# Two inputs also laid out features by tokens, and the memory's norm moved behind its projections

## What is computed

```python
for l in range(DEPTH):                                   # DEPTH = 2
    x = x + hybrid_mixer(rms_norm(x, norm_mix[l]), w_in[l], ...)
    x = x + memory_cross_attention(rms_norm(x, norm_mem_q[l]),
                                   rms_norm(mem, norm_mem_kv[l]), w_mem_q[l], w_mem_kv[l], w_mem_o[l])
    x = x + conv_ffn(rms_norm(x, norm_ffn[l]), ...)
# memory_cross_attention: q = h @ w_q; k, v = split(mem_n @ w_kv); softmax(q k^T) v @ w_o
# rms_norm(x, g) = x * rsqrt(mean(x*x) + 1e-6) * g
```

## Time and profile before

| what | us |
|---|---|
| median of 3 runs | 1925.69 |
| lowest, highest | 1925.57, 1926.07 |
| profiled execution, device time | 1925.96 |
| its span, first to last instruction | 1924.1 |
| PE busy in the span | 1901.3 |
| DVE, ACT, POOL busy | 1436.3, 1158.2, 397.0 |

### The profile page before, as it was taken

The page is one execution under the profiler, slowest core; times in us unless marked ns, Lnnn a source line. Parts: engine busy times, 40 slices in busy tenths (PEclk is TensorE's granted clock), DMA queues, the critical chain, the costliest instruction groups (busy, mean ns, idle before and its releaser), DMA issues.

```text
span 1924.1 us, 30347 instructions
## 1 busy us (share of the span) xinstructions
PE 1901.3 (99%) x11612; PEld 1656.2 (86%) x11612; DVE 1436.3 (75%) x2539; ACT 1158.2 (60%) x2120; POOL 397.0 (21%) x442
## 2 busy tenths in 40 slices
PE   9999999999999999999999999999999999999999
PEld 8878998887899988888887788888888898878887
DVE  5866986576698759875786978866885677888874
ACT  6666765565677546555667556555554666756552
POOL 1110222011012103420122204411440102122430
PEclk9999999999999999999999999999999999999999
DMA  8434556543455655655552355555565544345553
GB/s 298 139 104 142 196 188 233 181 134 124 140 165 193 201 187 176 195 191 172 189 173 99 111 164 197 192 191 184 189 193 191 187 155 151 105 137 182 191 190 128
DMA packets 90689, 329.93 MB, mean 171 GB/s; under 512 B 10032, under 2 KB 10416, under 8 KB 90288
## 3 DMA queue, kind: packets, MB, share of 16 engines
q1 hardware_dynamic: 90544, 327.98, 51.8%
HBM read 326.89 MB, written 1.05 MB: 170 GB/s over the span
## 4 chain that ended last, share of the span: by engine, by line
PE 86%; DVE 7%; ACT 4%; issue 1%; DMA 1%; SPq 0%; POOL 0%; DVEq 0%; ACTq 0%
PE PS L83 84%; PE PS L86 2%; DVE WL L98 2%; ACT TMP L95 2%; ACT WH L92 1%; DVE TMP L108 1%; DVE SM L114 1%; DMA RAW<-wts 1%; DVE X L98 0%; DVE SM L108 0%; ACT M L92 0%; ACT TMP L92 0%; DVE SM L98 0%; ACT M L95 0%; SPq L80 0%
## 5 line engine op out<-in xcount | busy, mean ns | idle before, releaser
L98 DVE TENSOR_TENSOR WL<-RAW,WH 128x1024 fp32r<-128x1024 f32 (+1 forms) x609 | 760.9, 1254 | 316.4 <-ACT WH L92 311.8
L92 ACT ACTIVATE WH<-RAW 128x1024 fp32r<-128x1024 f32 (+1 forms) x609 | 640.4, 1055 | 319.1 <-PE PS L83 312.9
L83 PE MATMUL PS<-WH,GX 128*128 128x512 f32 (+1 forms) x1632 | 525.0, 392 | 5.0 <-DVE GX L98 4.9
L83 PE MATMUL PS<-HX,WH 128*128 128x512 f32 (+1 forms) x1920 | 526.2, 344 | 3.2 <-DVE HX L108 1.5
L83 PE MATMUL PS<-GX,WH 128*128 128x256 f32 (+1 forms) x2176 | 453.7, 301 | 1.6 <-DVE WL L98 0.8
L83 PE MATMUL PS<-HX,WL 128*128 128x256 f32 x1488 | 417.8, 281 | 0.0
L83 PEld LDWEIGHTS PS<-HX,WH 128*128 128x128 f32 x1920 | 332.7, 189 | 50.1 <-DVE WL L98 2.1
L83 PEld LDWEIGHTS PS<-GX,WH 128*128 128x128 f32 x2176 | 350.8, 191 | 19.4 <-issue 1.2
L83 PEld LDWEIGHTS PS<-WH,GX 128*128 128x128 f32 x1632 | 305.7, 188 | 69.6 <-DVE WL L98 3.3
L83 PE MATMUL PS<-GX,WL 128*128 128x256 f32 x1264 | 356.5, 282 | 0.0
L83 PE MATMUL PS<-WL,GX 128*128 128x512 f32 (+1 forms) x816 | 316.7, 388 | 0.0
(11 more groups left out here) (142 smaller groups left out, 1667.8 us busy)
## 6 DMA issues: line engine op xcount, KB each, us to landing
RAW<-wts SPq DMA_DIRECT2D x607, 512.0 KB, 4.3
M<-bias SPq DMA_DIRECT2D x4, 512.0 KB, 11.2
M<-bias SPq DMA_DIRECT2D x1, 2048.0 KB, 9.0
X<-x SPq DMA_DIRECT2D x2, 512.0 KB, 5.6
TMP<-mem SPq DMA_DIRECT2D x1, 1024.0 KB, 11.9
out<-X SPq DMA_DIRECT2D x4, 256.0 KB, 3.4
CST<-cst SPq DMA_DIRECT2D x1, 714.0 KB, 9.6
RAW<-wts SPq DMA_DIRECT2D x2, 256.0 KB, 5.1
```

What stands on the lines that cost most here:

```text
L83: return Issued(self.eng and self.eng.matmul(o, l, r, start=first, stop=last, skip_group_check=share))
L92: return Issued(self.eng.activation(o, i, f, scale=scale))
L98: return Issued(self.eng and self.eng.tensor_tensor(o, a, b, op))
```

## The change

The host gives two more arrays. `xt` holds the first norm's gains (8 columns) and x features by tokens. `memt` holds the memory features by tokens. The core loads `xt` in two parts into TMP, and ACT and DVE make the high and low parts of the first projection's input from it. x itself is still loaded, later, for the residual and the squares. PE's transposes of x before the first projection and of the memory are gone, and PE starts with 16 matmuls on zeros instead of 8 and 12. In the first tile the products with the high weights come ahead of those with the low weights. `memt` is loaded straight into MEMX, without its norm. The memory by tokens goes to another place (MEMT in M), is squared during the values' step, and its factor RM comes from a Newton iteration of its own (`memory_norm`) in the stretch of gq. In both layers PE spreads RM over the partitions by two transposes just before mk0, DVE copies them to RB after `rotated_scales`, and `memory_key` is now a product with RB on DVE. The memory's values are scaled by RM in ACT's copy. The order of the first loads is changed too.

```diff
@@ dve_program
-            def first_norms():
+            def memory_norm():

                 e.wait_ge(squared, ("mem", 1, 1))
-                e.wait_ge(small)
-                e.tt(smc(0, 2), SS[:, 0:3:2], SS[:, 1:4:2], ALU.add).then_inc(small)
-                e.tt(smc(2, 2), SS[:, 8:11:2], SS[:, 9:12:2], ALU.add).then_inc(small)
...
-                y = newton(4)
...
+                mean_square(8)
+                e.copy(RM, newton(2)).then_inc(small, "rm")
...
@@ pe_program, block1
-                    occupy(4)
-                    e.wait_ge(id_in, 0)
-                    turn_x(("mix", 0), 0, lambda c, t: (x_in[c], 0))
-                    occupy(6)
-                    fm_four([("nq", 0, m) for m in range(4)], mix, ("mix", 0), lambda c, t: (x_in[c], 0))
+                    occupy(8)
+                    fm_four([("nq", 0, m) for m in range(4)], mix, None, None)
...
-                if L == 0:
-                    for k in range(0, KD, 2):
-                        ps = take(("memt", k // 2), WHOLE)
...
+                    e.wait_ge(small, "rm")
+                    put_over(("rm", L), [RM[:, t:t + 1].to_broadcast([128, 128]) for t in range(2)], WT + STB)
                     fm_tile(("mk", L, 0), mkv, WT + STB)
...
@@ act_program, block1
+                    def high_in(k):
+                        e.wait_ge(xt_in[k // 4], 0)
+                        e.act(ACT.Copy, H(0, k), XT[:, k, :], scale=XG[:, k:k + 1]).then_inc(ahi, (("mix", 0), k))
...
+                    for k in range(4, 8):
+                        high_in(k)
+                    highs_to(4)
                     for c in range(2):
                         squares(("mix", 0), c, lambda c, t: (x_in[c], 0))
+                    e.wait_ge(cst_in, 0)
...
-                    memory_key(0)
...
@@ dve_program, block1
-                e.copy(MK[:, m, :], bank(key)[:, 0:S]).then_inc(dout, key)
+                e.tt(MK[:, m, :], bank(key)[:, 0:S], RB[:, :], ALU.mult).then_inc(dout, key)
...
+                        if n == 1 and L == 0:
+                            memory_norm()
                     lows(("mk", L, 0))
                     rotate_queries(0)
                     yield
                     lows(("mk", L, 1))
                     rotate_queries(1)
                     rotated_scales()
+                    e.wait_ge(spread, ("rm", L))
+                    e.copy(RB[:, :], bank(("rm", L))[:, 0:S]).then_inc(dout, ("rm", L))
                     lows(("mk", L, 2))
+                    e.wait_ge(dout)
+                    memory_key(0)
                     lows(("mk", L, 3))
+                    memory_key(1)
                     yield
...
                 fill.rest()
+                memory_key(2)
+                memory_key(3)
...
@@ sp_program
-            e.dma(X[:, :, 0:512], x[:, :, 0:512]).then_inc(x_in[0], 0)
-            e.dma(CST[:, 0:C_COS], cst[:, 0:C_COS]).then_inc(id_in, 0)
+            e.dma(TMP[:, 0:1032], xt[:, 0:1032]).then_inc(xt_in[0], 0)
             e.dma(RAW[:, 0, 0:512], wts[0, :, 0:512]).then_inc(first_in, 0)
             e.dma(RAW[:, 0, 512:1024], wts[0, :, 512:1024]).then_inc(raw[0], 0)
-            e.dma(X[:, :, 512:1024], x[:, :, 512:1024]).then_inc(x_in[1], 0)
             half(1)
-            half(2)
-            e.dma(PAR[:, P_CW:P_N], par[:, P_CW:P_N]).then_inc(par_in, 0)
-            e.dma(CST[:, C_COS:C_N], cst[:, C_COS:C_N]).then_inc(cst_in, 0)
-            half(3)
-            e.dma(MEMT, mem).then_inc(mem_in, 0)
-            half(4)
+            e.dma(TMP[:, 1032:2056], xt[:, 1032:2056]).then_inc(xt_in[1], 0)
+            for h in range(2, RAWS):
+                half(h)
+            for c in range(2):
+                e.dma(X[:, :, c * 512:c * 512 + 512], x[:, :, c * 512:c * 512 + 512]).then_inc(x_in[c], 0)
             for h in range(RAWS, 2 * UNITS):
                 half(h)
+                if h == RAWS:
+                    e.dma(CST[:, :], cst).then_inc(cst_in, 0)
+                if h == RAWS + 3:
+                    e.dma(MEMT, mem).then_inc(mem_in, 0)
+                if h == RAWS + 5:
+                    e.dma(MEMX, memt).then_inc(memt_in, 0)
+                if h in (RAWS + 1, RAWS + 4, RAWS + 6, RAWS + 8):
+                    q = (RAWS + 1, RAWS + 4, RAWS + 6, RAWS + 8).index(h)
+                    e.dma(BIAS[:, 2 * q:2 * q + 2, :], bias[0, :, 2 * q:2 * q + 2, :]).then_inc(pair_bias_in[q], 0)
```

More of the change, by code:

```diff
@@ L143, in rest, with build @@
             pass
-def build(nc, x, mem, wts, wdt, bias, par, cst, gf, out):
+def build(nc, x, xt, mem, memt, wts, wdt, bias, par, cst, gf, out):
     with ExitStack() as ctx:
@@ L532, in fm_four @@
                             rms_over(st, over)
+                        if at[0] == 0:
+                            for i in range(4):
+                                ah, al, made_by = acts[i]
+                                e.wait_ge(ahi, made_by)
+                                e.wait_ge(hi, "first")
+                                e.mm(ps[0], WH[:, 0, i * 128:i * 128 + 128], ah, i == 0, False)
+                                e.wait_ge(alo, made_by)
+                                e.mm(ps[0], WH[:, 0, i * 128:i * 128 + 128], al, False, False)
                         for i in range(4 * part, 4 * part + 4):
@@ L722, in block1 @@
                 fm_tile(("nk", L, 0), mix)
+                if L == 0:
+                    e.wait_ge(cst_in, 0)
                 rms_over(("mix", L))
                 fm_tile(("nk", L, 1), mix, (0, 1, 2, 5, 6))
-                if L == 0:
-                    for k in range(0, KD, 2):
-                        ps = take(("memt", k // 2), WHOLE)
[L728 to L732, removed]
                 def turn_queries(q):
@@ L1204, in block1, with memory_squares @@
                 highs(("nk", L, 1))
[L1205 to L1211, removed]
+                def memory_squares(t):
+                    e.wait_ge(mem_in, 0)
+                    for c in range(2):
+                        e.wait_ge(squared)
+                        e.act(ACT.Square, junk(c), MEMT[:, t, c * 512:c * 512 + 512],
+                              acc=SS[:, 8 + 2 * t + c:9 + 2 * t + c]).then_inc(squared, ("mem", c, t))
                 def keys_out():
@@ L1255, in others @@
                         highs((("v", L), i))
+                        if L == 0 and i in (6, 7):
+                            memory_squares(i - 6)
                         yield
+                    if L == 0:
+                        e.wait_ge(squared, ("mem", 1, 1))
                     values_out(("v", L), V1, 0, ("rx", ("mix", L)))
@@ L1293, in block1 @@
                 fill.rest()
-                memory_key(2)
-                memory_key(3)
                 rotated_queries(0)
@@ L1320, in values @@
                         e.wait_ge(tile, (("mv", L), t))
-                        i = e.act(ACT.Copy, MV[:, t, :], bank((("mv", L), t))[:, :])
+                        i = e.act(ACT.Copy, MV[:, t, :], bank((("mv", L), t))[:, :], scale=RM[:, t:t + 1])
                         if t == 0:
@@ L1839, in block1, with low_in @@
                 if L == 0:
+                    def low_in(k):
+                        e.wait_ge(ahi, (("mix", 0), k))
+                        e.stt(Lw(0, k), XT[:, k, :], XG[:, k:k + 1], H(0, k).bitcast(F32), ALU.mult, ALU.subtract).then_inc(
+                            alo, (("mix", 0), k))
                     for k in range(4):
[L1841 to L1848 removed]
+                        low_in(k)
+                    for o in (0, 512):
+                        e.wait_ge(hi, 0 if o else "first")
+                        e.tt(WL[:, 0, o:o + 512], RAW[:, 0, o:o + 512], WH[:, 0, o:o + 512].bitcast(F32),
+                             ALU.subtract).then_inc(lo, 0 if o else "first")
+                    e.half = 1
+                    lows_to(1)
                     for k in range(4, 8):
[L1850 removed]
+                        low_in(k)
                     lows_to(4)
[L1852 to L1855 removed]
+                    norm(("mix", 0))
+                    e.wait_ge(cst_in, 0)
                 else:
```

71 lines of the change are left out of this document (26 added, 45 removed).

## The result

The changed kernel takes **1933.17 us** (median of 6 runs, 1932.66 to 1934.06), the kernel before beside it 1925.79 us (6 runs, 1925.57 to 1928.06). The ratio is 1.0033, 95% interval 1.0023 to 1.0043: slower by more than the 0.2% that can be told from no change. The forecast was 1928.2 us, "same", with a range up to 1930.4. The profiled run took 1932.66 us, its span is 1930.9, 6.8 more than before.

The account below looks back on a forecast made before the run. TensorE was taken as the bound, busy 1901.3 of 1924.1 us. Front -5.8, layer 1's tail +2.8 and layer 0's +5.5 gave +2.5 us on 1925.96, 1928.5, as median 1928.2 us; range 1923.8 to 1930.4.

Parts of the forecast that it names:

- The front: Start up to the attention's first scores: they begin at 27.5 instead of 33.34 us, 5.8 us off; half 1 stalls some 1.7.
- the third rival: Loads at the front's end: half 7 comes 1.5 to 2 us late, giving 1930.0 us; chance 0.15.
- The tail: End of neighbourhood attention: DVE's longer list and later bank releases add 5.5 us in layer 0, 2.8 in layer 1.
- The gaps named: TensorE waits before spread, mk1, mk2, mk3 in layer 0, and mk2, mk3 in layer 1, released by DVE, mk3's by RB.
- The first rival: Tail in both layers: waits hidden, only the two spreads' 0.5 us left, giving 1920.4 us; chance 0.09.
- the second: Front gains 6.4 us or more and gqa's rounds give back a third of the tail's 8.3: 1924.9 us; chance 0.16.
- costs nothing in the front: the memory's four squares: Squares on ACT in v's step: DVE's maxima about 1 us later, probabilities turned more than 4 us later, so no cost.
- In stages that I take for unchanged: Stages behind gqa: no time lost there; a loss would show the prediction wrong.
- My sum: Whole kernel: -5.8 + 2.8 + 5.5 = +2.5 us on the profiled 1925.96, median 1928.2 us; chance 0.60.
- every wait that it adds to TensorE costs its full length: Whole kernel, TensorE busy 1901.3 of 1924.1 us: each added wait counts at its own length.

Follow-up runs that it names:

- c1_before: The kernel before the change, unchanged, run again on another chip: 1928.84 us.
- e5: Changed kernel with the memory multiplied by its norm once on GpSimd, no key products on DVE, the norm's spread within the values' step: 1931.96 us.
- e13: Changed kernel with the memory multiplied by its norm once on GpSimd, spread behind the value projection, norm on DVE ahead of the low part: 1924.25 us, ratio 0.9981.
- e7: Changed kernel with the Newton iteration of the memory's norm run twice, 11 more small DVE instructions: 1934.97 us.
- e4: Changed kernel with memory's squares and norm early, the spread in its own bank, and RB's copy ahead of the key products: 1925.07 us, ratio 0.9983.
- e10: Changed kernel with only the memory's squares moved from steps 6 and 7 of the values to steps 0 and 1: 1932.48 us, ratio 1.0024.
- c3_after: The changed kernel, unchanged, run beside e12 on the same chip: 1933.59 us.
- e12: Changed kernel with idle TensorE products, 1 ahead of mk2 and 4 ahead of mk3 in both layers: 1932.18 us.
- e2: Changed kernel with the spread of the memory's factor in a free score bank instead of the ring of four: 1931.8 us, ratio 1.0026.
- c4_three: The kernel of e4 again, unchanged, beside e13 on the same chip: 1925.57 us, ratio 0.9984.
- e1: Changed kernel with the memory's squares in values' steps 0 and 1 and its norm on DVE in step 3: 1928.74 us, ratio 1.0007.
- c2_after: The changed kernel, unchanged, on the same chip as the other experiments: 1933.36 us, ratio 1.0028.

## Why the prediction was wrong

- **The front: right.** Forecast 27.5 us for the first scores and 5.8 off; 27.29 and 6.05 measured (6.2 against c1_before). Half 1 waits 1.24 us, not 1.7. Its wait varied over 0.7 to 1.9 us from run to run, with a fall of the clock in e5 (1.73) and e13 (1.93). The loads kept 409 to 415 GB/s over 10 to 40 us, so the third rival (late loads) didn't come, and the figure of about 358 GB/s per core in the Trainium skill ("DMA: Bandwidth & Descriptors", Specifications), there a stack's 716 GB/s divided by its two cores, is no limit for the one core that loads here: the measurement decides.
- **The tail: right in size and place.** Forecast 5.5 and 2.8, measured 5.50 and 3.04. The gaps named (0.9, 1.6, 0.8, 2.0 and 0.65, 2.0) came as 0.75, 1.25, 0.65, 1.82 and 0.52, 1.80, with the releasers named. e7 shows the norm's list counts in full; e4 takes most of the tail away. The first rival (tail hidden) falls by these rows, the second by the steps: gqa gave nothing back.
- **The step that failed first: "costs nothing in the front: the memory's four squares".** The text put DVE's maxima off by about 1 us and set 4 us of slack against it, until that pair's probabilities are turned. The maxima come 1.8 us late (3.0 us behind their scores, 1.2 in the kernel before and in e10), since DVE's low part ahead of them waits for the late high part. ACT's exponentials (46.95) follow, and behind these in ACT's order stands a copy of the pair before (its second turned probabilities, 50.41), which the first weighing needs. That was the nearer deadline: in the kernel before the copy ends at 55.24 us and the weighing starts at 56.26, 1.0 us of slack. TensorE waited 0.81 us. 0.92 us in all, shown by e10.
- **"In stages that I take for unchanged" nothing was to be lost.** 2.1 us were, in a stage whose instructions are the same. It belongs to no instruction of the change: the kernel before shows it too (c1_before). This is the largest single piece of what the sum lacks. My sum stood on one profiled run at the quick pace, and the medians of the first comparison set a kernel mostly at the quick pace (five of six runs) against one at the slow. What decides it is open, and so is whether the change shifts the odds.
- **The clock behind the new waits was no term at all.** The text says that "every wait that it adds to TensorE costs its full length", and counts it at that and no more. Where the granted clock falls behind it, 1.5 us come on top (c3_after); with the waits filled the median is 1.4 us less (e12). The profiled run that I compared with had no fall, so it is seen in medians only: on the other chips they stand 5.0 and 5.5 apart, the landmarks 3.7.
- **Sum.** Forecast +2.5. Landmarks at equal pace: +3.7, that is 0.35 better in front, 0.9 worse at the squares, 0.25 in layer 1 and 0.4 in small shifts that I didn't trace. The pace adds 2.1. Of the 1.6 that are left of the 7.4 between the medians, the profiled run has 1.0 in its long last store. For the other runs it stays open: a fall of the clock (1.5) doesn't fit the four of six whose mean clock is 1.000.

## What to carry to other kernels

When a ring of buffers serves several tiles in turn, one more tile shifts every release behind it: write the ring out with its releases before placing it, and mend all late releases of the chain together. An edit that only gathers several waits into one (e2, 2.65 us) can win in waits and lose it again to the clock. A wait of TensorE costs more than its length when the granted clock falls behind it, so give new waits near 2 us an upper end 1.5 us higher. Before explaining a difference of 2 us, look whether the kernel before has two levels of its own.

## What the runs showed of the hardware

- A stage of matmuls without waits ran at one of two steady paces, 346.7 or 353.3 ns for a pair of 768 columns, at a granted clock of 1.00, fixed for 110 us from its restart on; two programs showed both (before and c1_before, e4 and c4_three).
- The granted clock fell behind waits of TensorE (1.73 us in e5, 1.80 in e1 and c3_after, 1.93 in e13) in some traces and not in others with the same wait (c2_after, 1.82 us). In the tail a fall cost 1.5 us (c3_after, e1). Falls near 1100 us (0.83 over 10 us in e12, 0.92 and 0.91 in c1_before) moved the last matmul by 0.2 us or less.
- A product of plain f32 operands 128x256 took 0.44 us of TensorE, four times the 0.11 to 0.12 of the kernel's fp32r operands of that size.
